# Twelve of sixteen input blocks through the seven products of a Strassen step, and a weight combination made by adding transfers

## The chip, the cores and the metric

The kernel runs on one core of one Trainium2 chip. The metric is the device time in microseconds of one execution; several are run and their median is taken. The core has a matrix engine (TensorE, PE in the profile), a vector engine (VectorE, DVE), an activation engine (ScalarE, ACT), GpSimd (POOL), and SyncE (SP), which here only issues transfers; 16 DMA engines carry them.

## The reference

Two layers over x (256 tokens by 2048 channels). Each has a mixer, a dense MLP and a gated per-layer embedding:

```python
def squared_relu_mlp(u, w1, w2):
    hdn = jnp.square(jax.nn.relu(jnp.einsum("bsd,df->bsf", u, w1)))
    return jnp.einsum("bsf,fd->bsd", hdn, w2)
...
    h = x
    for i in range(DEPTH):
        ...
        h = h + m                       # mixer A (layer 0) or B (layer 1)
        h = h + squared_relu_mlp(rmsnorm(h, norm_mlp[i]), mlp_w1[i], mlp_w2[i])
        h = h + per_layer_embedding(h, p[i], norm_ple[i], ple_w_proj[i], ple_w_gate[i])
    return rmsnorm(h, norm_final)
```

D_MODEL is 2048, D_FF 8192, SEQ 256, all in float32. The change concerns the product u @ w1 of both layers' MLPs.

## The kernel before

**Precision by splitting.** Every float32 weight tile is split into a high part (float32r) and the rest: ScalarE copies the tile into `whi` (line 1044), VectorE subtracts that from the tile into `wlo` (line 1559), and TensorE multiplies three times, high by high, high by low and low by high (`three`, lines 711 to 713). A weight tile of two blocks (256 rows by 512 columns) is called a slot here; `whi` and `wlo` are rings of four slots. TensorE counts `slot_used` up after each slot, ScalarE may write slot i only when TensorE has finished slot i - 4, VectorE follows ScalarE (`slot_hi`), TensorE follows VectorE (`slot_lo`). All engines go through the slots in the same order, which is written out by hand.

**The MLP.** The hidden dimension is cut into 8 chunks of 1024 columns. Chunk 0 of u @ w1 is computed in two plain blocks of 8 half-steps each (`up.b` and `up.b + 1`). Then 7 steps (`FIRST`, then `STEP` six times) each compute the next chunk of u @ w1 and, in the same slots, the down product of the previous chunk with w2; `END` does the last down product. With two layers there are 14 such steps.

**Seven products.** In a step, the 2 by 2 arrangement (two token halves; two halves of the input blocks; two halves of the chunk's columns) of 8 of the 16 input blocks goes through Strassen's seven products in Winograd's form. A slot `("m", of, part)` is product `of` with the weight blocks 2*part and 2*part + 1: 2 blocks of one token half, 6 matmuls. The other 8 input blocks go in `("r", column half, part)`, and the down products in `("d", column block, part)` and `("e", 3, part)` (the last column block of the chunk before): 2 blocks of both token halves, 12 matmuls. `STEP` has 38 slots: 14 "m", 12 "d", 4 "e", 8 "r", which is 372 matmuls of 128x512. `FIRST` has 34 slots, without the "e".

**Weight combinations.** Products 5, 6, 7 and 4 need sums of the four quarters of w1's chunk. The quarters lie in `raw` as four fields, loaded with 1 MB each by `field`; VectorE makes each combination in place, part by part (`weight_sum`, line 1570), at a slot that `sums_after` gives: eight instructions of 128x1024 a step. All other slots are loaded by `plain` into a ring of four buffers `pl`, each reload waiting for the `slot_lo` of its last use.

**What VectorE has beside the split.** Before a slot's split, `run_step` places other work by the slot's index: the turned hidden blocks (`turn_hidden`, index `HIDDEN1` and `hidden_before`), the low part of hidden operands (`HI0`, `HI1`), the addition of a finished down column block to `h` (`add_down`, 4 slots after its last slot), and `mix` (4 instructions on PSUM, lines 1577 to 1583), 5 slots after the last of products 6 and 7:

```python
                        if i == t.at("d", j, 3) + SLOTS:
...
                            add_down(base + t.at("d", j, 3) + 1, j)
                    if i == corners_done(t) + SLOTS + 1:
                        mix(t, base, n)
...
                slot_low(layer, k, parity, i, raw[:, FIELD[of], 2 * part:2 * part + 2, :] if kind == "m" else
...
                for later in t.sums_after(i):
                    weight_sum(t, n, later)
```

**Combinations of u.** Four sums of the input blocks are made once a layer by `combine` in `run_mlp`, between the slots of `up.b + 1`: `whole` (high and low parts added up, line 1640, 128x2048), four sums of 128x512, their high parts on ScalarE and the low parts on VectorE. The low parts of `up.b` and `up.b + 1` come from line 1388, their matmuls from lines 678 to 680.

Of the kernel before, what the change touches and what calls it, by code (L numbers as in the profile page):

```python
# [36 lines left out]
SP_TILES = 4  # L37
LATE = (("d", 2, 0), ("m", 2, 0), ("d", 2, 1), ("m", 2, 1), ("d", 2, 2), ("d", 2, 3),
        ("m", 4, 0), ("r", 0, 0), ("m", 4, 1), ("r", 0, 1), ("r", 0, 2), ("r", 0, 3),
        ("m", 3, 0), ("r", 1, 0), ("m", 3, 1), ("r", 1, 1), ("r", 1, 2), ("r", 1, 3))  # L40
FIRST = (("m", 1, 0), ("m", 1, 1), ("d", 0, 0), ("d", 0, 1), ("m", 5, 0), ("d", 1, 0), ("m", 5, 1), ("d", 1, 1),
         ("m", 7, 0), ("m", 6, 0), ("m", 7, 1), ("d", 0, 2), ("d", 0, 3), ("m", 6, 1), ("d", 1, 2), ("d", 1, 3)) + LATE
# [13 lines left out]
SUMS = (5, 6, 7, 4)  # L56
FIELD = {1: 0, 5: 0, 6: 0, 4: 0, 7: 1, 3: 2, 2: 3}
COMBO = {5: 0, 6: 1, 7: 2, 3: 3}
BANK = {1: 0, 2: 0, 7: 1, 4: 1, 5: 2, 3: 2, 6: 3}
IN_PLACE_AFTER = {5: 1, 6: 5, 7: None, 4: 6}  # L60
OUT_ADD, OUT_TURN = (17, 19), (17, 21)
HI0, HI0_END, HIDDEN1, HI1, HI1_FIRST, HI1_END = 6, 4, 3, 12, 11, 12
# [7 lines left out]
class Table:  # L70


    def __init__(self, slots):
        self.slots = tuple((s + (None,))[:4] for s in slots)
        plain = [s[:3] for s in self.slots if s[0] != "m"]
        self.loads = tuple(dict.fromkeys(plain))
        self.load = tuple(None if s[0] == "m" else self.loads.index(s[:3]) for s in self.slots)
# [20 lines left out]
FIRST, STEP, END = Table(FIRST), Table(STEP), Table(END)  # L98

# [5 lines left out]
def field_freed(t):  # L105
    return t.at("m", 4, 1), t.at("m", 7, 1), t.at("m", 3, 1), t.at("m", 4, 1)
# [1962 lines left out]
```

## Time and profile before

| | us |
|---|---|
| median of 3 runs | 2232.65 (2230.52 to 2233.39) |
| the profiled execution, its own time | 2228.94 |
| its span | 2227.2 |
| TensorE busy | 2204.0 (99%) |
| VectorE busy | 1720.9 (77%) |
| ScalarE busy | 1243.1 (56%) |
| granted TensorE clock, mean | 0.998 |
| DMA | 503.56 MB, 226 GB/s over the span |

Busy time is that in which an engine runs an instruction. A matmul's row gives 0.39 us, but matmuls overlap: the next one starts 0.23 us later, and it is the distance between starts that adds up. The same holds in a small way on VectorE: an instruction of 1.22 us is followed by the next 1.13 to 1.14 us after its start.

### The profile page before, as it was taken

What the parts mean: (1) busy time and instruction counts of PE and PEld (TensorE: products, weight loads), DVE (VectorE), ACT (ScalarE), POOL (GpSimd) and SP (SyncE); (2) the same over time, 40 slices, a digit from 0 to 9 for tenths busy, and PEclk for the clock granted to TensorE, in tenths of its full rate; (3) what the DMA queues carried; (4) which work ended last, traced back from release to release, by engine and by line L of the source; (5) the groups of instructions that cost most, each with busy time, mean ns of one, the idle gap of its engine ahead of it and who ended that gap; (6) DMA issues with size and microseconds to landing.
All of it is one profiled execution on the core that took longest, in us unless ns stands there. A gap on an engine that the chain in (4) does not pass through costs nothing.

```text
span 2227.2 us, 29440 instructions
## 1 busy us (share of the span) xinstructions
PE 2204.0 (99%) x10152; PEld 1832.7 (82%) x10152; DVE 1720.9 (77%) x1897; ACT 1243.1 (56%) x1542; POOL 156.9 (7%) x183
## 2 busy tenths in 40 slices
PE   8999999999999999999999999999999999999998
PEld 7998688888888888887888888888888888888876
DVE  6999868787787787767766667688877877877676
ACT  5666656556556556456744444565564554654565
POOL 3888000000000000000000000000000000000000
PEclk9999999999999999999999999999999999999999
DMA  9544498768677677688876777777776776776783
GB/s 341 171 152 152 140 317 245 242 210 243 222 212 242 219 216 236 223 230 256 236 251 194 244 239 218 251 237 253 214 239 219 216 235 218 224 227 224 232 263 139
DMA packets 499528, 503.56 MB, mean 226 GB/s; under 512 B 261040, under 2 KB 299120, under 8 KB 498416
## 3 DMA queue, kind: packets, MB, share of 16 engines
q1 hardware_dynamic: 497600, 499.71, 72.3%
q10 hardware_dynamic: 1696, 1.67, 0.2%
q8 instruction: 50, 0.82, 0.2%
q0 software_dynamic: 144, 1.05, 0.1%
q14 instruction: 38, 0.31, 0.0%
HBM read 464.62 MB, written 37.75 MB: 226 GB/s over the span
## 4 chain that ended last, share of the span: by engine, by line
PE 75%; DVE 4%; DMA 3%; ACT 1%; issue 1%; SPq 1%; DVEq 0%; ACTq 0%
PE acc L711 14%; PE acc L713 13%; PE acc L712 13%; PE acc L678 7%; PE acc L680 7%; PE acc L679 7%; PE tp L711 4%; PE tp L713 4%; PE tp L712 4%; DMA pT<-staged 2%; DVE wlo L1559 1%; DMA staged<-prows 1%; SPq L430 1%; DVE prows L1473 1%; DVE wlo L1388 1%
## 5 line engine op out<-in xcount | busy, mean ns | idle before, releaser
L1044 ACT ACTIVATE whi<-pl 128x1024 fp32r<-128x1024 f32 x372 | 386.5, 1049 | 303.1 <-PE acc L713 207.0
L1559 DVE TENSOR_TENSOR wlo<-pl,whi 128x1024 fp32r<-128x1024 f32 x372 | 442.8, 1205 | 142.5 <-ACT whi L1044 137.1
L1388 DVE TENSOR_TENSOR wlo<-raw,whi 128x1024 fp32r<-128x1024 f32 x248 | 296.4, 1220 | 128.7 <-ACT whi L939 125.3
L939 ACT ACTIVATE whi<-raw 128x1024 fp32r<-128x1024 f32 x248 | 255.8, 1054 | 198.2 <-PE acc L680 186.4
L1044 ACT ACTIVATE whi<-raw 128x1024 fp32r<-128x1024 f32 x196 | 207.3, 1058 | 184.6 <-PE acc L713 121.7
L1559 DVE TENSOR_TENSOR wlo<-raw,whi 128x1024 fp32r<-128x1024 f32 x196 | 238.5, 1219 | 54.8 <-ACT whi L1044 51.1
L678 PE MATMUL acc<-whi,b_hi 128*128 128x512 f32 x672 | 262.4, 390 | 2.1 <-DVE wlo L1388 1.6
L679 PE MATMUL acc<-wlo,b_hi 128*128 128x512 f32 x672 | 261.5, 389 | 0.0
L680 PE MATMUL acc<-whi,b_lo 128*128 128x512 f32 x672 | 261.5, 389 | 0.0
L711 PE MATMUL acc<-whi,a_hi 128*128 128x512 f32 x596 | 232.3, 390 | 0.6 <-DVE wlo L1559 0.6
L711 PE MATMUL acc<-whi,b_hi 128*128 128x512 f32 x596 | 232.2, 390 | 0.7 <-DVE wlo L1559 0.7
L713 PE MATMUL acc<-whi,b_lo 128*128 128x512 f32 x596 | 231.9, 389 | 0.0
L712 PE MATMUL acc<-wlo,a_hi 128*128 128x512 f32 x596 | 231.9, 389 | 0.0
L713 PE MATMUL acc<-whi,a_lo 128*128 128x512 f32 x596 | 231.9, 389 | 0.0
L712 PE MATMUL acc<-wlo,b_hi 128*128 128x512 f32 x596 | 231.9, 389 | 0.0
L678 PEld LDWEIGHTS acc<-whi,b_hi 128*128 128x128 f32 x672 | 126.2, 188 | 30.2 <-issue 3.2
L680 PEld LDWEIGHTS acc<-whi,b_lo 128*128 128x128 f32 x672 | 126.2, 188 | 26.4
L679 PEld LDWEIGHTS acc<-wlo,b_hi 128*128 128x128 f32 x672 | 126.2, 188 | 26.2 <-issue 0.2
L1570 DVE TENSOR_TENSOR raw<-raw 128x1024 f32<-128x1024 f32 x112 | 136.1, 1215 | 0.0
L711 PEld LDWEIGHTS acc<-whi,b_hi 128*128 128x128 f32 x596 | 111.9, 188 | 25.4 <-DVE wlo L1559 1.4
L711 PEld LDWEIGHTS acc<-whi,a_hi 128*128 128x128 f32 x596 | 111.9, 188 | 25.4 <-DVE wlo L1559 1.5
L713 PEld LDWEIGHTS acc<-whi,b_lo 128*128 128x128 f32 x596 | 111.9, 188 | 23.3
(218 smaller groups left out, 4049.7 us busy)
## 6 DMA issues: line engine op xcount, KB each, us to landing
pl<-in_mlp_w SPq DMA_DIRECT2D x368, 512.0 KB, 5.0
raw<-in_mlp_w SPq DMA_DIRECT2D x72, 1024.0 KB, 6.0
raw<-in_sc_w_in SPq DMA_DIRECT2D x48, 1024.0 KB, 6.4
raw<-in_cf_w_pw SPq DMA_DIRECT2D x64, 512.0 KB, 8.7
raw<-in_ple_w_gate SPq DMA_DIRECT2D x32, 1024.0 KB, 7.4
staged<-prows SPq DMA_DIRECT2D x240, 128.0 KB, 3.3
pT<-staged SPq DMA_DIRECT2D x56, 512.0 KB, 5.8
raw<-in_cf_w_pw SPq DMA_DIRECT2D x16, 1024.0 KB, 7.4
```

The source lines that it names most:

```text
L430: nc.sync.dma_start(rows[:, :, i * Q:(i + 1) * Q], turned[i * Q:(i + 1) * Q, :, :]).then_inc(staged_ready, 16)
L678: nc.tensor.matmul(o, xhi[:, k, s], hi, start=first and c == 0, stop=False)
L679: nc.tensor.matmul(o, xhi[:, k, s], lo, start=False, stop=False)
L680: mm = nc.tensor.matmul(o, xlo[:, k, s], hi, start=False, stop=last and c == 1)
L711: nc.tensor.matmul(o, xhi, hi, start=start, stop=False, skip_group_check=again)
L712: nc.tensor.matmul(o, xhi, lo, start=False, stop=False, skip_group_check=again)
L713: return nc.tensor.matmul(o, xlo, hi, start=False, stop=stop, skip_group_check=again)
L939: nc.scalar.activation(whi[:, e % SLOTS, :, :], raw[:, e // 2, 2 * (e % 2):2 * (e % 2) + 2, :], ACT.Copy).then_inc(hi_ready, 1)
L1044: nc.scalar.activation(whi[:, ring(parity, i), c, :], source[:, c, :], ACT.Copy).then_inc(slot_hi, 1)
L1388: nc.vector.tensor_tensor(wlo[:, e % SLOTS, :, :], raw[:, e // 2, 2 * (e % 2):2 * (e % 2) + 2, :], whi[:, e % SLOTS, :, :].bitcast(F32), A ...
L1559: nc.vector.tensor_tensor(wlo[:, ring(parity, i), c, :], source[:, c, :], whi[:, ring(parity, i), c, :].bitcast(F32), ALU.subtract).then_i ...
L1570: nc.vector.tensor_tensor(o, x, y, ALU.subtract).then_inc(slot_sum, 1)
```

## The change

Twelve of the 16 input blocks go through the seven products (`SP_TILES` from 4 to 6: three parts for each product), four are left for "r". A `STEP` then has 42 slots: 21 "m", 13 "d" (the last down tile is given as two single slots of 6 matmuls each), 4 "e", 4 "r". The order is written anew. w1's quarters are loaded in parts of 512 KB into `raw` (the last part into `vpad`); the fourth quarter comes through the plain ring. The signs are turned so that each combination is a running addition: 5 is b11 + b12 (VectorE), 6 adds b22 to it, 4 adds b21 (VectorE), 7 is b12 + b22 (VectorE). The addition for product 6 is made by three transfers of 512 KB a step that GpSimd issues with an adding write (`add_block`), each after the split of product 5's slot; ScalarE waits for them (`t2_ready`). `whole` is 128x3072 now and is made in `up.b` after its first split (`gather`); the sums of u are 128x768, their high and low parts are made in pieces. `mix` keeps its four instructions with other signs, and its place by rule: 5 slots after the last of products 6 and 7.

```diff
-SP_TILES = 4
-LATE = (("d", 2, 0), ("m", 2, 0), ("d", 2, 1), ("m", 2, 1), ("d", 2, 2), ("d", 2, 3),
-        ("m", 4, 0), ("r", 0, 0), ("m", 4, 1), ("r", 0, 1), ("r", 0, 2), ("r", 0, 3),
-        ("m", 3, 0), ("r", 1, 0), ("m", 3, 1), ("r", 1, 1), ("r", 1, 2), ("r", 1, 3))
...
-STEP = (("m", 1, 0), ("e", 3, 0), ("m", 1, 1), ("e", 3, 1), ("m", 5, 0), ("e", 3, 2), ("m", 5, 1), ("e", 3, 3),
-        ("d", 0, 0), ("m", 6, 0), ("d", 0, 1), ("m", 6, 1), ("d", 0, 2), ("d", 0, 3),
-        ("d", 1, 0), ("m", 7, 0), ("d", 1, 1), ("m", 7, 1), ("d", 1, 2), ("d", 1, 3)) + LATE
+SP_TILES = 6
+SP_PARTS = SP_TILES // 2
+LATE = (("m", 2, 0), ("d", 2, 0), ("m", 2, 1), ("d", 2, 1), ("m", 2, 2), ("d", 2, 2),
+        ("m", 4, 0), ("d", 2, 3), ("m", 4, 1), ("r", 0, 0), ("m", 4, 2), ("r", 0, 1),
+        ("m", 3, 0), ("r", 1, 0), ("m", 3, 1), ("r", 1, 1), ("m", 3, 2))
+FIRST = (("m", 1, 0), ("m", 1, 1), ("d", 0, 0), ("m", 1, 2), ("d", 0, 1), ("m", 5, 0), ("d", 1, 0), ("m", 5, 1),
+         ("d", 1, 1), ("m", 5, 2), ("m", 7, 0), ("m", 7, 1), ("m", 7, 2), ("d", 0, 2), ("m", 6, 0), ("d", 0, 3),
+         ("m", 6, 1), ("d", 1, 2), ("m", 6, 2), ("d", 1, 3, 0), ("d", 1, 3, 1)) + LATE
+STEP = (("m", 1, 0), ("e", 3, 0), ("m", 1, 1), ("e", 3, 1), ("m", 1, 2), ("e", 3, 2), ("m", 5, 0), ("e", 3, 3),
+        ("m", 5, 1), ("d", 0, 0), ("m", 5, 2), ("d", 0, 1), ("m", 7, 0), ("d", 1, 0), ("m", 7, 1), ("d", 1, 1),
+        ("m", 7, 2), ("d", 0, 2), ("m", 6, 0), ("d", 0, 3), ("m", 6, 1), ("d", 1, 2), ("m", 6, 2),
+        ("d", 1, 3, 0), ("d", 1, 3, 1)) + LATE
...
-SUMS = (5, 6, 7, 4)
...
+SUMS = (5, 7, 4)
...
-HI0, HI0_END, HIDDEN1, HI1, HI1_FIRST, HI1_END = 6, 4, 3, 12, 11, 12
+HI0, HI0_END, HIDDEN1, HI1, HI1_FIRST, HI1_END = 8, 4, 3, 15, 13, 12
...
-            if i == max(n - 3, 0 if user is None else self.at("m", user, part)):
+            if i == (self.at("m", 2, part) if of == 4 else max(n - 3, 0 if user is None else self.at("m", user, part))):
...
 def corners_done(t):
-    return max(t.at("m", 6, 1), t.at("m", 7, 1))
+    return max(t.at("m", 6, SP_PARTS - 1), t.at("m", 7, SP_PARTS - 1))
...
 def hidden_before(t):
-    return t.at("r", 0, 3) + SLOTS
+    return t.at("r", 0, 1) + SLOTS
...
+            def field(layer, k, f, part):
+
+                row, col = (SP_TILES if f == 2 else 0) * P + part * 2 * P, NB if f else 0
...
+                nc.sync.dma_start(field_part(f, part), t_in["mlp_w1"][layer][row:row + 2 * P, bass.ds(col, NB)]
+                                  .rearrange("(c r) n -> r c n", r=P)).then_inc(field_ready[f][part], 16)
...
-                free = freed(layer, k, i)
+                    kind, of, part, _ = t.slots[i]
+                    free = freed(layer, k, i) + (t.slots[i][:2] == ("m", 2))
...
+                    if kind == "m" and of in LAST_USE:
+                        sp.wait_ge(slot_lo, free)
+                        if then is not END:
+                            field(layer, k + 1, LAST_USE[of], part)
...
+                elif of == 6:
+                    act.wait_ge(t2_ready[part], 16 * n + 16)
...
             def weight_sum(t, n, i):
 
                 _, of, part, _ = t.slots[i]
...
+                b11, b12, b22 = (field_part(f, part) for f in range(3))
+                b21 = pl[:, t.load[t.at("m", 2, part)] % 4, :, :]
+                o, more, needs = {5: (b11, b12, 1), 7: (b12, b22, 2), 4: (b11, b21, None)}[of]
+                if needs is not None:
+                    dve.wait_ge(field_ready[needs][part], 16 * n + 16)
+                nc.vector.tensor_tensor(o, o, more, ALU.add).then_inc(slot_sum, 1)
...
+                def gather(e):
+                    if e == 0:
+                        dve.wait_ge(operand_ready, 2 * prev.o + 6)
...
+                        steps.mark(nc.vector.tensor_tensor(whole, X[u][0][:, 0:2 * SP_TILES, :].bitcast(F32),
+                                                           X[u][1][:, 0:2 * SP_TILES, :].bitcast(F32), ALU.add))
...
-                run_behind(up.b, Result(prev, BLOCKS - 1), X[u], ROW_MLP + layer, (NORM_MLP[layer], up.s))
+                run_behind(up.b, Result(prev, BLOCKS - 1), X[u], ROW_MLP + layer, (NORM_MLP[layer], up.s), gather)
...
+            def add_block(layer, k, part):
+
+                row, col = (SP_TILES + 2 * part) * P, (k + 1) * 2 * NB + NB
+                pool.wait_ge(slot_lo, first_slot(layer, k) + slots_of(k).at("m", 5, part) + 1)
+                nc.gpsimd.dma_start(field_part(0, part), t_in["mlp_w1"][layer][row:row + 2 * P, col:col + NB]
+                                    .rearrange("(c r) n -> r c n", r=P), accum_op=ALU.add).then_inc(t2_ready[part], 16)
```

## Rows read from the trace of the kernel before

**Rows 1.** The page, busy time of each engine.

```profile
PE 2204.0 (99%) x10152; PEld 1832.7 (82%) x10152; DVE 1720.9 (77%) x1897; ACT 1243.1 (56%) x1542; POOL 156.9 (7%) x183
```

**Rows 2.** Waits of TensorE: line, what it waited for, us in total, times, longest.

```profile
PE acc L678 <- DVE wlo L1388: 4.7, 6, 1.7
...
PE acc L711 <- DVE wlo L1559: 1.4, 2, 0.7
```

**Rows 3.** One STEP: us; busy PE, PEld, DVE, ACT, POOL; clock, DMA share, GB/s.

```profile
574.72:659.39 84.67, 84.65 (x373) 69.67 (x373) 67.57 (x62) 47.39 (x50) 0.00 (x0) 1.00 0.73 224
```

**Rows 4.** Groups of VectorE in that window: the weight combinations.

```profile
L1570 DVE TENSOR_TENSOR raw<-raw 128x1024 f32<-128x1024 f32 x8 | 9.7, 1211 | 0.0
```

**Rows 5.** Timeline of TensorE: first matmul of three slots (m, d, m and on).

```profile
568.20 0.39 PE L711 MATMUL tp<-whi,b_hi 128*128 128x512 f32 x1
...
570.92 0.39 PE L711 MATMUL acc<-whi,s_hi 128*128 128x512 f32 x1
...
572.28 0.39 PE L711 MATMUL tp<-whi,b_hi 128*128 128x512 f32 x1
```

**Rows 6.** Timeline of ScalarE, the same place.

```profile
572.48 1.06 ACT L1044 ACTIVATE whi<-raw 128x1024 fp32r<-128x1024 f32 x1 [0.30 <-PE acc L713]
```

**Rows 7.** Timeline of VectorE around a mix.

```profile
573.58 1.23 DVE L1559 TENSOR_TENSOR wlo<-raw,whi 128x1024 fp32r<-128x1024 f32 x1
574.72 0.68 DVE L1577 TENSOR_TENSOR work<-acc,work 128x512 f32<-128x512 f32 x1
...
577.38 1.22 DVE L1559 TENSOR_TENSOR wlo<-pl,whi 128x1024 fp32r<-128x1024 f32 x1
578.51 1.22 DVE L1588 TENSOR_TENSOR h<-tp,h 128x1024 f32<-128x1024 f32 x1
579.64 1.22 DVE L1559 TENSOR_TENSOR wlo<-raw,whi 128x1024 fp32r<-128x1024 f32 x1
```

**Rows 8.** Timeline of TensorE: a wait in layer 0's FIRST, and the matmul after.

```profile
396.69 0.47 PE L711 MATMUL acc<-whi,b_hi 128*128 128x512 f32 x1 [0.74 <-DVE wlo L1559]
396.99 0.40 PE L712 MATMUL acc<-wlo,b_hi 128*128 128x512 f32 x1
```

**Rows 9.** Timeline of VectorE at that wait.

```profile
395.32 2.36 DVE L1559 TENSOR_TENSOR wlo<-pl,whi 128x1024 fp32r<-128x1024 f32 x2
```

**Rows 10.** Timeline of VectorE at the start of a STEP: the split of slot 3.

```profile
622.96 1.17 DVE L1559 TENSOR_TENSOR wlo<-pl,whi 128x1024 fp32r<-128x1024 f32 x1
```

**Rows 11.** Timeline of TensorE: the start of that slot 3.

```profile
624.29 0.40 PE L711 MATMUL tp<-whi,b_hi 128*128 128x512 f32 x1
```

**Rows 12.** Timeline of VectorE at the start of layer 0's MLP.

```profile
328.72 3.50 DVE L1388 TENSOR_TENSOR wlo<-raw,whi 128x1024 fp32r<-128x1024 f32 x3 [0.47 <-ACT whi L939]
...
338.26 4.63 DVE L1388 TENSOR_TENSOR wlo<-raw,whi 128x1024 fp32r<-128x1024 f32 x4 [1.24 <-ACT whi L939]
...
351.00 2.28 DVE L1640 TENSOR_TENSOR pl<-a_hi,a_lo 128x2048 f32<-128x2048 f32 x1
```

**Rows 13.** Timeline of TensorE there: the half-steps 0 and 3 of up.b.

```profile
330.09 0.47 PE L678 MATMUL acc<-whi,a_hi 128*128 128x512 f32 x1 [0.27 <-DVE wlo L1388]
...
339.63 0.47 PE L678 MATMUL acc<-whi,a_hi 128*128 128x512 f32 x1 [1.10 <-DVE wlo L1388]
```

**Rows 14.** Timeline of VectorE at the start of layer 1's MLP.

```profile
1449.91 1.23 DVE L1431 TENSOR_TENSOR res<-acc,h 128x1024 f32<-128x1024 f32 x1 [0.34 <-PE acc L680]
...
1454.64 3.50 DVE L1388 TENSOR_TENSOR wlo<-raw,whi 128x1024 fp32r<-128x1024 f32 x3 [1.24 <-ACT whi L939]
```

**Rows 15.** DMA issues on the page: KB each, median us from issue to landing.

```profile
pl<-in_mlp_w SPq DMA_DIRECT2D x368, 512.0 KB, 5.0
...
emb_kept<-emb SPq DMA_DIRECT2D x8, 512.0 KB, 12.4
```

**Rows 16.** Landing times of the loads by line 530 in two windows: 569 to 590, and 612.5 to 615.

```profile
DMA to landing us min/median/max: 3.6/4.4/5.4
...
DMA to landing us min/median/max: 6.6/7.1/7.5
```

More of the change, by code:

```diff
@@ L70, with __init__ @@
 class Table:
-    def __init__(self, slots):
+    def __init__(self, slots, single_loads=False):
         self.slots = tuple((s + (None,))[:4] for s in slots)
-        plain = [s[:3] for s in self.slots if s[0] != "m"]
-        self.loads = tuple(dict.fromkeys(plain))
-        self.load = tuple(None if s[0] == "m" else self.loads.index(s[:3]) for s in self.slots)
+        keys = [None if s[0] == "m" and s[1] != 2 else s if single_loads else s[:3] + (None,) for s in self.slots]
+        self.loads = tuple(dict.fromkeys(key for key in keys if key is not None))
+        self.load = tuple(None if key is None else self.loads.index(key) for key in keys)
         self.freed = tuple(max(i for i, n in enumerate(self.load) if n == m) for m in range(len(self.loads)))
@@ L387, in trunk @@
         u2_ready, u3_ready, mixed = sem("u2_ready"), sem("u3_ready"), sem("mixed")
+        t2_ready = [sem(f"t2_ready{p}") for p in range(SP_PARTS)]
         up_free, down_free = sem("up_free"), sem("down_free")
@@ new lines, in plain @@
+            def plain(layer, k, n, free=None):
+                kind, of, part, single = slots_of(k).loads[n]
+                tiles = slice(0, 2) if single is None else slice(single, single + 1)
+                down = kind in "de"
+                w = t_in["mlp_w2" if down else "mlp_w1"][layer]
+                row, col = (((k - (kind == "e")) * 2 * NB, of * NB) if down else
+                            (2 * SP_TILES * P, (k + 1) * 2 * NB + of * NB) if kind == "r" else (SP_TILES * P, (k + 1) * 2 * NB))
+                row, rows = row + (2 * part + tiles.start) * P, (tiles.stop - tiles.start) * P
+                src = (w[bass.ds(row, rows), col:col + NB] if down else w[row:row + rows, bass.ds(col, NB)]
+                       ).rearrange("(c r) n -> r c n", r=P)
@@ L563, in load_step @@
                         take_back(c1)
-                        if t is FIRST:
-                            field(layer, 0, 3)
                     if i == hidden_before(t) - 1:
@@ L1642, in combine @@
+                def combine(e):
+                    if e == 0:
                         steps.wait()
-                        a11, a12, a21, a22 = (whole[:, k:k + TILES, s:s + P] for s in (0, P) for k in (0, TILES))
-                        s1, s2, s3, s4 = (combos[:, i, :, :] for i in range(4))
-                        steps.mark(nc.vector.tensor_tensor(s1, a21, a22, ALU.add))
-                        nc.vector.tensor_tensor(s3, a11, a21, ALU.subtract)
+                        steps.mark(nc.vector.tensor_tensor(s1, a21, a22, ALU.subtract))
@@ L1894, in short_taps @@
                 dve.wait_ge(vpad_ready, 32 * j + 32)
+                dve.wait_ge(const_ready, 4)
                 for k in range(WB):
@@ L2043, in _ @@
             nc.gpsimd.dma_start(bias2, t_in["cf_b_pw2"][0].partition_broadcast(P)).then_inc(bias2_ready, 16)
+            def add_block(layer, k, part):
[3 more added lines that the diff above has]
+                                    .rearrange("(c r) n -> r c n", r=P), accum_op=ALU.add).then_inc(t2_ready[part], 16)
+            for layer in range(DEPTH):
+                for k in range(STEPS):
+                    for part in range(SP_PARTS):
+                        add_block(layer, k, part)
+                if layer == 0:
+                    pool.wait_ge(slot_lo, first_slot(0, STEPS))
+                    nc.gpsimd.memset(vpad[:, :, 0:PAD], 0.0).then_inc(const_ready, 1)
 _INS = ["x", "p", "norm_mix", "norm_mlp", "norm_ple", "cf_w_pw1", "cf_b_pw1", "cf_w_dw", "cf_b_dw",
```

167 lines of the change are left out of this document (90 added, 77 removed).

## Prediction

> **What bounds the kernel now.** I read the busy times first, to see whether one engine fills the span: TensorE is busy 2204.0 of 2227.2 us [rows 1]. Then TensorE's waits, to see what the rest is: it waits 1.4 us in all in the MLP's slots [rows 2]. So a matmul taken away there is worth its full distance, if the slots still come in time. Then one STEP by itself: 84.67 us, clock 1.00, VectorE busy 67.57 of them, ScalarE 47.39, DMA share 0.73 [rows 3]. VectorE is second, with 17 us to spare over 38 slots; what counts is whether they lie where they are needed, since TensorE can run no more than three slots ahead of a late split. Last the timelines, for distances. An "m" slot takes 1.36 us and a "d" slot 2.72, six and twelve times 0.2267 [rows 5]. ScalarE starts a slot 0.20 us after TensorE ends the slot four before it, VectorE's split starts 1.30 us after that end [rows 5 to 7]. TensorE starts 1.37 us after the start of its split: 338.26 to 339.63 and 395.32 to 396.69 [rows 8, 9, 12, 13]; a wait also costs about 0.09 us more, as the second matmul comes after 0.30 and not 0.23 us [rows 8]. Back to back, VectorE's split, combination or addition to h takes 1.135 us (577.38, 578.51, 579.64), and a mix 2.66 us (574.72 to 577.38) [rows 7].
>
> **The matmuls.** "m" goes from 14 to 21 slots (84 to 126 matmuls), "r" from 8 to 4 (96 to 48): 372 to 366 in a STEP, 324 to 318 in FIRST. Six times 0.2267 is 1.36 us a step, 14 steps: -19.0 us.
>
> **VectorE and ScalarE over a step.** Slots go from 38 to 42, but two are halves (one instruction of 512 elements is 0.68 us, line 1577 in [rows 7]). VectorE: two full splits more (2.3), two halves (1.2), combinations from 8 [rows 4] to 6, because product 6's are taken away (2 x 1.135 fewer), and the third parts of 5, 7 and 4 (3 x 1.135 more). That is 40 full and 2 half splits, 9 combinations: in all about +4.6 us, 72 of 83 us. ScalarE gains some 3.3 us and stays near 51. Neither is full on average, so this costs nothing by itself.
>
> **Where VectorE's work falls.** The rule "mix 5 slots after the last corner" now puts it elsewhere. In the new STEP, ("m",6,2) is slot 22; 23 and 24 are half slots, 25 is ("m",2,0), 26 "d", 27 ("m",2,1), 28 "d". Four slots of 1.36 us in a row follow one another just ahead of the mix (27). Take TensorE's start of slot 22 as 0; without waits it starts 25 at 4.08, 26 at 5.44, 27 at 8.16, 28 at 9.52, 29 at 12.24. VectorE can begin slot 25's split at 1.30 (slot 21 ended at 0). Then, each 1.135: split 25; combination for product 4, part 0 (new place: behind ("m",2,part)) at 2.44; split 26 at 3.57 (TensorE can start at 4.94, in time); mix from 4.71 to 7.37; split 27 at 7.37, so TensorE starts it at 8.74 and not 8.16; combination part 1 at 8.50; addition of down block 1 (`add_down`, 4 slots after slot 24) at 9.64; split 28 at 10.77, so TensorE starts it at 12.14. Slot 27 would have been over at 10.10. TensorE falls back 0.58 and then 2.04, together 2.62, plus 0.09 of restart: **2.7 us a step**. Afterwards split 29 at 11.9, combination, split 30 at 14.2 are in time for 14.9 and 16.2. FIRST has the same slots there (mix at 23, addition at 24), so it pays the same. Fourteen times 2.7 is +37.8 us. Before, the mix stood among "d" slots and the row shows VectorE going on without a wait of TensorE [rows 2, 7].
>
> The neighbours of this place bound it. Below: ScalarE runs ahead and doesn't matter; if VectorE's chain of 9.47 us (seven instructions and the mix, less the overlap that the starts already hold) were 2.6 us shorter, nothing would be lost. Above: the same, if a load is late too (below).
>
> **The start of a step** is the other dense stretch. It already runs at the edge: split 3 starts at 622.96, TensorE its slot 3 at 624.29, 1.33 later [rows 10, 11]. In the new order VectorE does 14 instructions from there to slot 11's split (8 splits, 4 combinations, a hidden operand, an addition): 622.96 + 15.9 + 1.37 = 640.2, and TensorE wants slot 11 at 624.29 + 16.32 = 640.6. To slot 15 it is 21 instructions: 648.2 against 648.8. It holds by 0.4 us: no cost, but no room. In FIRST the four "m" in a row (slots 9 to 12) give VectorE a backlog that reaches slot 13 about 0.5 us late; before it was 0.7 at slot 11 [rows 8]. I count that as even. The end of a step (hidden block at slot 40) has the same m, r, m cover ahead of it as before.
>
> **The start of the MLP.** `gather` puts `whole` between splits 0 and 1 of up.b. For 2048 elements it took 2.28 us [rows 12]; for 3072 that makes 3.4. In layer 0 VectorE is already late there: TensorE starts half-step 0 at 330.09, right behind its split (328.72), and waits 1.10 us at half-step 3 [rows 12, 13]. Everything to split 3 moves by 3.4, less some 0.1 of gaps: **+3.3 us**. Behind it nothing makes this good, as TensorE is the bound. In layer 1 the block before ends at about 1449.7, when VectorE's addition starts, and split 3 at 1454.64 is needed only at 1449.7 + 8.16 - 1.37 = 1456.5 [rows 14]; the addition is pushed back by about 0.9 us, which is hidden. The later sums of u (four of 768, their low parts in pieces) cost VectorE about what the old ones did.
>
> **The adding transfers.** Product 5's part is split about 11 us into a STEP, and product 6's is needed by ScalarE at about 30 and at the latest at 34: 19 to 23 us for 512 KB; in FIRST it is 12 to 15. The trace has no adding transfer. From below it is a plain load of that size, 5.0 us, from above the copy of `emb` out, 12.4 us [rows 15]. It reads its target too, so I take about 8. All of this is hidden, so +0. The Trainium skill, "DMA: Bandwidth & Descriptors", section "Anatomy of one DMA — SWDGE (gpsimd) path", gives 2.0 us plus bytes over 436 GB/s, an estimate of 3.2 us here; the load row's 5.0 is more, and by either the sum is the same.
>
> **GpSimd** is idle in the MLP (156.9 us busy in all, [rows 1]); its queue holds only these issues, and each waits for a split that comes anyway.
>
> **SP and the buffers.** Nine field parts replace four 1 MB loads. Around the dense place a reload waits for its slot's split: ("m",2,2)'s load goes out when split 26 is done (4.8), ("d",2,3)'s when split 28 is done (12.0); the latter lands at 12.1 + L, is copied, split, and lets slot 32 start at about 14.7 + L, wanted at 20.3. It is in time for L up to 5.6. Loads in the same part of the old step landed in 3.6 to 5.4 [rows 16]: +0.
>
> **Sum.** -19.0 + 37.8 + 3.3 = +22.1 us. The profiled execution's own time is 2228.94, span 2227.2: it becomes 2251.0. The median of the runs, 2232.65, lies 3.7 above it, so I say **2254.7, about 2254 us**, slower by 1%.
>
> **Rivals.** A change within 0.2% (4.5 us) could hardly be told from none.
>
> 1. The cut is realised. The burst at slots 25 to 28 is absorbed, because VectorE's distances are shorter there, or TensorE has more lead than I give it. Needed: the chain to split 28 ends by 8.15 and not 10.77. Then -19.0 + 3.3: 2217. For it: before, no STEP shows a wait. Against: the distances are those of rows of the same instructions.
> 2. Half of the burst is absorbed (1.3 us a step instead of 2.7): 2232.65 - 19.0 + 18.2 + 3.3 = 2235, between 2225 and 2245.
> 3. The transfers become the bound at the same place. The adding ones bring 1.57 MB more to 84.67 x 224 = 19.0 MB, or twice that if the target's read counts: share 0.73 x 84.67 = 61.8 us busy, plus 5 to 10, over 86: 0.78 to 0.84. If loads then land as slowly as those beside the staged exchange, 7.1 us and up to 8 [rows 16], ("d",2,3) is 1.5 to 2.4 us late each step: 21 to 34 us more, 2276 to 2288. Against it: the adding transfers run in the first half of the step, the tight loads in the second. The Trainium skill, same page, section "Issuing engines are not separate DMA queues", says that transfers of all issuers share the same 16 engines; by that rule GpSimd's queue brings no relief, and no run here shows it yet.
> 4. An adding transfer takes over 23 us: each step waits at product 6. At 12.4 this is far off; beyond 2290.
>
> **Chances.** Forecast 0.60 (own range 2245 to 2265); rival 1 0.13; rival 2 0.11; rivals 3 and 4 0.16. The range 2230 to 2286 leaves out rival 1, a part of rival 2 and the end of 3 and 4, about 0.2. Slower: 0.60 + 0.16 + half of rival 2 = 0.81; same 0.04; faster 0.15.
>
> **What would show it.** Right: TensorE waits on line 1559's successor about 14 to 28 times, twice a step at ("m",2,1) and the "d" behind it, 2.6 us a step; the distance from mix to mix near 86.0 us; VectorE without a gap from ("m",2,0) to split 28; layer 0's up.b with a wait of about 1.7 us at half-step 1 and 2.9 at half-step 3. Wrong: steps of 83.3 us; ScalarE waiting for a transfer, by name, at product 6 or at `pl`; or waits of TensorE at slots 4 to 15, which would say that the start of the step is the tighter place.

## Result: slower by 1.6%, and the profile after

The changed kernel took 2266.95 us (median of 4 runs, 2258.89 to 2275.96), the kernel before 2232.3 us beside it (4 runs, 2230.52 to 2233.39): a ratio of 1.0157 [1.0108, 1.0206]. It is slower, as forecast, and within the range of 2230 to 2286, but 13 us above the forecast of 2254, and 2 us outside the band of 2245 to 2265 that had got a chance of 0.60. The change cost 34.7 us and not 22.1. Its runs also spread over 17 us, those of before over 3. The profiled execution is the slowest of the four (2275.96 us), so its trace shows more trouble than the median has.

The page of the changed kernel: busy times, the queues that are new or will matter, and the issues of the adding transfers (KB each, median us to landing). The answers to [rows 1] and [rows 15]:

```profile
span 2274.2 us, 29838 instructions
...
PE 2205.6 (97%) x10068; PEld 1820.6 (80%) x10068; DVE 1790.1 (79%) x1975; ACT 1289.4 (57%) x1606; POOL 207.2 (9%) x226
...
q0 software_dynamic: 11568, 23.07, 5.6%
...
q8 instruction: 59, 0.97, 0.2%
...
pl<-in_mlp_w SPq DMA_DIRECT2D x340, 512.0 KB, 5.1
...
raw<-in_mlp_w POOLq DMA_DIRECT2D x42, 512.0 KB, 9.5
```

The waits of TensorE (line, what for, us in total, times, longest), which answer to [rows 2]:

```profile
PE acc L730 <- DVE wlo L1593: 37.8, 34, 3.7
PE acc L697 <- DVE wlo L1422: 9.0, 6, 2.7
PE acc L732 <- issue: 3.3, 1, 3.3
```

84 matmuls are gone and TensorE is busy for no less time (2205.6 us, before 2204.0). It now waits 37.8 us for VectorE's splits in the slots, where it waited 1.4. And once it stands for 3.3 us though nothing that the profile shows is missing.

One step, from mix to mix (columns as in [rows 3]); VectorE's timeline around the mix (start, us, as in [rows 7]); and TensorE's two waits there:

```profile
426.02:511.74 85.72, 83.61 (x367) 68.46 (x366) 71.93 (x67) 50.46 (x55) 3.56 (x3) 1.00 0.82 239
```

```profile
593.99 1.23 DVE L1593 TENSOR_TENSOR wlo<-pl,whi 128x1024 fp32r<-128x1024 f32 x1 [2.46 <-ACT whi L1068]
595.13 1.22 DVE L1605 TENSOR_TENSOR raw<-raw,pl 128x1024 f32<-128x1024 f32 x1
596.27 1.22 DVE L1593 TENSOR_TENSOR wlo<-pl,whi 128x1024 fp32r<-128x1024 f32 x1
597.40 0.68 DVE L1612 TENSOR_TENSOR work<-acc,work 128x512 f32<-128x512 f32 x1
...
600.06 1.21 DVE L1593 TENSOR_TENSOR wlo<-pl,whi 128x1024 fp32r<-128x1024 f32 x1
601.19 1.22 DVE L1605 TENSOR_TENSOR raw<-raw,pl 128x1024 f32<-128x1024 f32 x1
602.33 1.22 DVE L1623 TENSOR_TENSOR h<-tp,h 128x1024 f32<-128x1024 f32 x1
603.46 2.35 DVE L1593 TENSOR_TENSOR wlo<-pl,whi 128x1024 fp32r<-128x1024 f32 x2
```

```profile
601.33 0.50 PE L730 MATMUL acc<-whi,a_hi 128*128 128x512 f32 x1 [0.31 <-DVE wlo L1593]
...
604.73 0.50 PE L730 MATMUL acc<-whi,b_hi 128*128 128x512 f32 x1 [1.74 <-DVE wlo L1593]
```

This is the forecast burst: from split 25 (593.99) to split 28 (603.46) VectorE has no gap, 9.47 us as worked out, and TensorE is late at slot 27 and again at slot 28. The step takes 85.7 to 85.8 us in place of 84.4 (the mean between the mixes of before), +1.34: 1.36 us fewer for six matmuls, 2.70 us more for the burst.

The start of layer 0's MLP, VectorE and TensorE (answers to [rows 12, 13]):

```profile
331.08 1.22 DVE L1422 TENSOR_TENSOR wlo<-raw,whi 128x1024 fp32r<-128x1024 f32 x1 [0.46 <-ACT whi L963]
332.22 3.35 DVE L1675 TENSOR_TENSOR pl<-a_hi,a_lo 128x3072 f32<-128x3072 f32 x1
...
343.89 2.36 DVE L1422 TENSOR_TENSOR wlo<-raw,whi 128x1024 fp32r<-128x1024 f32 x2 [1.25 <-ACT whi L963]
```

```profile
336.86 0.47 PE L697 MATMUL acc<-whi,a_hi 128*128 128x512 f32 x1 [1.40 <-DVE wlo L1422]
...
345.26 0.47 PE L697 MATMUL acc<-whi,a_hi 128*128 128x512 f32 x1 [2.73 <-DVE wlo L1422]
```

From split 0 to split 3 it is 12.81 us, before 9.54: +3.27, forecast 3.3.

**What the forecast did not have.** The hidden operand is written out and read back turned (`pT<-staged`). In layer 0's FIRST it comes back late: the transfer's landing time (the queue from 393.9 to 394.6), then ScalarE, then TensorE:

```profile
pT<-staged SPq DMA_DIRECT2D x1, 512.0 KB, 11.1
```

```profile
405.26 1.06 ACT L1021 ACTIVATE b_hi<-pT 128x1024 fp32r<-128x1024 f32 x1 [4.40 <-DMA pT<-staged]
```

```profile
408.92 0.77 PE L730 MATMUL acc<-whi,b_hi 128*128 128x512 f32 x1 [3.74 <-DVE wlo L1593]
409.49 0.63 PE L731 MATMUL acc<-wlo,b_hi 128*128 128x512 f32 x1
409.91 0.63 PE L732 MATMUL acc<-whi,b_lo 128*128 128x512 f32 x1
...
411.62 0.46 PE L730 MATMUL acc<-whi,b_hi 128*128 128x512 f32 x1
```

The return was issued at 394.11 and used at 405.26, eleven us later. Layer 1's FIRST has the same again: the return lands in 11.0 us, ScalarE waits 2.7 us for it, and TensorE then waits 2.1:

```profile
1538.90 1.06 ACT L1021 ACTIVATE a_hi<-pT 128x1024 fp32r<-128x1024 f32 x1 [2.74 <-DMA pT<-staged]
```

```profile
1542.57 0.47 PE L730 MATMUL acc<-whi,a_hi 128*128 128x512 f32 x1 [2.09 <-DVE wlo L1593]
```

After the wait at 408.92 the matmuls come every 0.43 us and not every 0.227: the clock's lower level, 1.2 GHz, for about 3 us. The same fall follows some other waits. Ahead of the last 10 us, the windows of 5 us in which the mean clock is below 0.97 begin in this trace at 15, at 405 and 410, at 1055, at 1910 and from 1940 to 1950; the trace of before has none but at its end. And in layer 1 one step took 95.3 us. In it (TensorE's timeline; the code queue from 1930 to 1950):

```profile
1941.38 0.49 PE L730 MATMUL acc<-whi,b_hi 128*128 128x512 f32 x1 [1.86 <-DVE wlo L1593]
...
1946.09 0.59 PE L732 MATMUL acc<-whi,b_lo 128*128 128x512 f32 x1 [3.29 <-issue]
1946.47 0.63 PE L730 MATMUL tp<-whi,a_hi 128*128 128x512 f32 x1
```

```profile
q8 instruction: 4, 0.07, 1.4%
```

TensorE stops ahead of the last matmul of a step's slot 0, when its inputs are there, in a stretch in which four packets of code arrive; then the clock is low to about 1950.7. The step is the first behind a jump back of TensorE's loop.

### The profile page after: what moved, and what is told of

It is laid out like the page before. It is cut to its first block, busy times and chain, and to the rows that moved or that the text cites. A ratio compares the mean times of both kernels' runs of the same rounds, so it can differ in the third digit from the quotient of the medians.

```text
span 2274.2 us, 29838 instructions
## 1 busy us (share of the span) xinstructions
PE 2205.6 (97%) x10068; PEld 1820.6 (80%) x10068; DVE 1790.1 (79%) x1975; ACT 1289.4 (57%) x1606; POOL 207.2 (9%) x226
## 4 chain that ended last, share of the span: by engine, by line
PE 62%; DVE 9%; DMA 7%; issue 3%; ACT 3%; SPq 1%; DVEq 0%; ACTq 0%
PE acc L730 11%; PE acc L732 11%; PE acc L731 11%; PE acc L697 6%; PE acc L698 6%; PE acc L699 6%; PE tp L730 3%; PE tp L732 3%; PE tp L731 3%; DVE wlo L1593 3%; DMA pT<-staged 3%; DMA staged<-prows 2%; SPq L442 1%; ACT whi L1068 1%; DVE raw L1605 1%
## 5 line engine op out<-in xcount | busy, mean ns | idle before, releaser
L1593 DVE TENSOR_TENSOR wlo<-pl,whi 128x1024 fp32r<-128x1024 f32 x372 | 431.5, 1165 | 155.6 <-ACT whi L1068 154.8
L1422 DVE TENSOR_TENSOR wlo<-raw,whi 128x1024 fp32r<-128x1024 f32 x248 | 296.8, 1220 | 129.6 <-ACT whi L963 126.1
L963 ACT ACTIVATE whi<-raw 128x1024 fp32r<-128x1024 f32 x248 | 255.8, 1054 | 194.7 <-PE acc L699 188.5
L1593 DVE TENSOR_TENSOR wlo<-raw,whi 128x1024 fp32r<-128x1024 f32 x238 | 289.8, 1220 | 21.1 <-ACT whi L1068 13.9
L1068 ACT ACTIVATE whi<-raw 128x1024 fp32r<-128x1024 f32 x238 | 251.3, 1057 | 82.8 <-PE acc L732 57.9
L699 PE MATMUL acc<-whi,b_lo 128*128 128x512 f32 x672 | 261.6, 389 | 0.0
L698 PE MATMUL acc<-wlo,b_hi 128*128 128x512 f32 x672 | 261.6, 389 | 0.0
L730 PE MATMUL acc<-whi,a_hi 128*128 128x512 f32 x568 | 223.9, 394 | 17.6 <-DVE wlo L1593 17.6
L732 PE MATMUL acc<-whi,b_lo 128*128 128x512 f32 x568 | 222.0, 391 | 3.3 <-issue 3.3
L732 PE MATMUL acc<-whi,a_lo 128*128 128x512 f32 x568 | 222.1, 391 | 0.0
L731 PE MATMUL acc<-wlo,a_hi 128*128 128x512 f32 x568 | 221.9, 391 | 0.0
L731 PE MATMUL acc<-wlo,b_hi 128*128 128x512 f32 x568 | 221.8, 391 | 0.0
L2100 POOL DMA_DIRECT2D raw<-in_mlp_w x42 | 50.1, 1193 | 1680.2 <-DVE wlo L1593 1680.2
L699 PEld LDWEIGHTS acc<-whi,b_lo 128*128 128x128 f32 x672 | 126.2, 188 | 26.2
L697 PE MATMUL acc<-whi,a_hi 128*128 128x512 f32 x320 | 125.6, 393 | 6.8 <-DVE wlo L1422 6.8
```

Of the source, the lines that this page charges most:

```text
L697: nc.tensor.matmul(o, xhi[:, k, s], hi, start=first and c == 0, stop=False)
L698: nc.tensor.matmul(o, xhi[:, k, s], lo, start=False, stop=False)
L699: mm = nc.tensor.matmul(o, xlo[:, k, s], hi, start=False, stop=last and c == 1)
L730: nc.tensor.matmul(o, xhi, hi, start=start, stop=False, skip_group_check=again)
L731: nc.tensor.matmul(o, xhi, lo, start=False, stop=False, skip_group_check=again)
L732: return nc.tensor.matmul(o, xlo, hi, start=False, stop=stop, skip_group_check=again)
```

## Experiments

Each is the changed kernel with the edit shown. Ratios are to the kernel before, run beside it on the same chip (2233.1 us for experiments 1 to 4, 2233.7 for 5 to 8, 2233.0 for 9 to 11, 2233.6 for 12). The changed kernel was run beside another 2232.3, so differences of two experiments from different groups carry about 1 us of that. Where "waits" or "steps" are given, they come from one profiled execution of each kernel.

**1. The addition later.**

```diff
-                            if i == t.at("d", j, 3) + SLOTS:
+                            if i == t.at("d", j, 3) + (2 * SLOTS if j == 1 else SLOTS):
```

> The changed kernel with one edit: the addition of down column block 1 to h stands 8 slots after its last slot (slot 32 of a STEP) and not 4 (slot 28). Theory A, VectorE's burst behind the mix sets the step: split 28 starts 1.135 us earlier, TensorE's second wait shrinks from 1.74 to about 0.6 us, the distance from mix to mix goes from 85.7 to 84.6 us, 14 x 1.13 = 16 us off the whole. Rival T, the transfers set it (ScalarE waits some 4 us a step for the load of product 2's last part): the distance stays at 85.7, as the load's time doesn't change. Rival C, what costs is the TensorE clock's fall after a wait: the gain would be more than 16 us and the spread of the runs would shrink.

2248.29 us (2241.97 to 2251.64), ratio 1.0067 [1.0055, 1.008]. Steps of 84.6 us, 1.15 less:

```profile
PE acc L730 <- DVE wlo L1593: 19.6, 32, 2.5
```

One instruction of VectorE (1.135 us), moved out of the burst by four slots, gives its own length back in each step. The burst sets the step, and there VectorE's time is TensorE's. By medians the gain is 18.7 us, a little more than 14 times 1.15, and the spread fell from 17 to 9.7 us, so rival C has a small part that this run can't exclude. The trace also has a step of 91.9 us, with a stand of 2.7 us.

**2. No adding transfers.** ScalarE's wait for them goes too. The kernel leaves b22 out of product 6, so it is for its time alone.

```diff
-                for k in range(STEPS):
-                    for part in range(SP_PARTS):
-                        add_block(layer, k, part)
```

> The changed kernel without the adding transfers: product 6 takes the combination of product 5 as it is (the output leaves out b22 in product 6). Theory A: the steps stay at 85.7 us from mix to mix. Of the first step of layer 0, which had a TensorE wait of 3.7 us for the staged exchange beside three adding transfers, the wait goes, with the slow clock after it: 4 to 6 us off in all, for both layers up to 8. Rival T: the steps themselves become shorter by 1 us or more, 14 us or more in all, and ScalarE's waits for pl fall from 8 us a step to near 3. If the adding transfers cost nothing at all, the time stays.

2258.03 us (2257.0 to 2259.21), 1.0117 [1.0102, 1.0132]. Steps of 85.7 to 85.8 us, as with them, so inside a step the transfers are hidden, as forecast. But the median is 8.9 us lower, more than theory A's 4 to 8, and the spread 2 us in place of 17 (four runs each). In FIRST the return lands in 6.8 us, in layer 1's in 5.6, and ScalarE finds the operand there, without a wait:

```profile
pT<-staged SPq DMA_DIRECT2D x1, 512.0 KB, 6.8
```

```profile
400.05 1.05 ACT L1021 ACTIVATE b_hi<-pT 128x1024 fp32r<-128x1024 f32 x1
```

**3. The gather later.**

```diff
-                    if e == 0:
+                    if e == 5:
```

> The changed kernel with the sum of high and low parts (128x3072) behind split 5 of up.b and not behind split 0. If its place costs what was forecast, TensorE's waits at half-steps 1 and 3 of layer 0's up.b (about 1.9 and 2.7 us) fall back to one of about 1.1 us: 3.3 us off, layer 1 unchanged. If something else of the start sets the time (the exchange that brings the last input blocks), the 3.3 us are waited for later and the time stays.

2261.78 us (2259.29 to 2265.71), 1.0138 [1.0123, 1.0153]: 5 us below the changed kernel's median, 0.4 us above its fastest run, so four runs each don't decide it. The trace says more: split 0 and split 3 lie 9.54 us apart again (329.14, 338.68), and the waits on line 1422 fall from 9.0 to 6.4 us. But a part of the delay has only moved. At its new place the gather (342.10, 3.35 us) holds up the low part of an operand, and TensorE waits for that:

```profile
350.22 0.50 PE L697 MATMUL acc<-whi,a_hi 128*128 128x512 f32 x1 [1.76 <-DVE a_lo L1527]
```

From the first matmul of line 697 to FIRST, TensorE takes 135.4 us, with the early gather 137.0, before 133.1: the move gives back about half of the 3.3 us (such a stretch differs by up to 1 us from trace to trace), and the rest is waited for at the new place. The low clock at 340 to 350, behind the wait of 2.7 us, stands in four of the seven traces with the early gather (not in the changed kernel's own) and in none of the five with the late one.

**4. A product ahead of the down load,** with edit 1. ("m",6,2) comes before ("d",1,2), and the mix six slots behind it, so a "d" slot more lies inside the burst.

```diff
-         ("m", 6, 1), ("d", 1, 2), ("m", 6, 2), ("d", 1, 3, 0), ("d", 1, 3, 1)) + LATE
+         ("m", 6, 1), ("m", 6, 2), ("d", 1, 2), ("d", 1, 3, 0), ("d", 1, 3, 1)) + LATE
...
-                        if i == corners_done(t) + SLOTS + 1:
+                        if i == corners_done(t) + SLOTS + 2:
```

> Three edits against the burst: the addition of e1; the last part of product 6 stands ahead of the down slot before it (slots 21 and 22 exchanged); the mix 6 slots after it (still slot 27). Theory A, worked out with the same distances: TensorE starts slot 27 on time and slot 28 about 0.1 to 0.2 us late, the distance from mix to mix is 83.5 us, 14 x 2.2 = 31 us off, which is about the time of the kernel before or 10 us below it. Rival T: the load of product 2's last part (issued behind split 26) or the next one is then what TensorE waits for, and the distance stays at 84.5 or more, with ScalarE's wait for pl ahead of TensorE's.

2242.36 us (2231.62 to 2255.98), 1.0052 [1.0029, 1.0075]. Steps of 83.7 us with one wait of 0.3 us:

```profile
PE acc L730 <- DVE wlo L1593: 8.5, 17, 2.1
```

The burst is gone and the fastest run is 1.5 us below the median of the kernel before, and yet this kernel's median is 11 us above its fastest run and the spread 24 us. Against the changed kernel the median fell by 24.6 us where 31 were expected. Something beside the burst and the gather costs, and not in every run.

**5. The combination by VectorE,** with no adding transfers (the edit of experiment 2 as well).

```diff
-SUMS = (5, 7, 4)
+SUMS = (5, 7, 6, 4)
...
-IN_PLACE_AFTER = {5: 1, 7: None, 4: 6}
+IN_PLACE_AFTER = {5: 1, 7: None, 6: 5, 4: 6}
...
-                o, more, needs = {5: (b11, b12, 1), 7: (b12, b22, 2), 4: (b11, b21, None)}[of]
+                o, more, needs = {5: (b11, b12, 1), 7: (b12, b22, 2), 6: (b11, b22, 2), 4: (b11, b21, None)}[of]
```

> The combination for product 6 is made by VectorE in place (b11 plus b22, three more 128x1024 additions a step, behind the splits of slots 15, 17 and 19), and the 42 adding transfers are gone; burst, order and the gather are as in the changed kernel. Theory A (the adding transfers buy VectorE time that it does not need: the step is set by TensorE and by the burst of slots 25 to 28, and the irregular 10 to 17 us come from the transfers): the sums lie in VectorE's slack, the distance between mixes stays 85.7 us, the wait of the first chunk's exchange goes, and the time is 2257 to 2262 us with a spread of under 4 us, as in the run without the adding transfers. Rival B (VectorE needs the relief: 3 x 1.13 = 3.4 us more work a step pushes the burst later): up to 14 x 3.4 = 48 us more, and at least 1 us a step, so 2272 us or more, with waits of TensorE on VectorE's splits at slots 17 to 21.

2262.71 us (2260.07 to 2266.75), 1.0127 [1.0112, 1.0142], steps of 85.7 to 85.8 us. VectorE does 42 instructions more (1834.3 us busy) and no step is longer: the relief that the transfers were to bring was not needed. Theory A missed one thing: the trace has a step of 94.7 us and a stand without any adding transfer.

```profile
PE acc L732 <- issue: 4.6, 1, 4.6
```

So that part does not need the transfers, and the small spread of experiment 2 says less than I had read in it. The return lands in 6.0 and 5.5 us here, and no FIRST has the long wait.

**6. All mends, sum by VectorE** (edits 1, 3, 4, 5).

> All mends together: the sum for product 6 by VectorE, no adding transfers, the gather behind split 5, addition 1 of the down product eight slots later, and load (m,6,2) before (d,1,2) with the mix six slots behind it. Theory A (the terms add): the burst costs 0.3 us a step in place of 2.05 and the gather 1 us in place of 3.3, so the time is the cut of 84 matmuls with little given back: 2214 to 2224 us, 0.4 to 0.8% below the kernel before, with a spread of under 4 us. Rival B (VectorE, at 85% and with three more additions in a step, is late again at slots 20 to 28): the step stays above 84.4 us and the time is 2232 us or more.

2232.76 us (2226.84 to 2242.89), 1.0005 [0.9993, 1.0017]: theory A's time is missed by 9 us. The profiled run, its fastest, has steps of 83.6 to 83.8 us, 0.72 below before, and no fall of the clock ahead of the end; the other runs lose up to 16 us more. But even this run is 3 us above theory A. Its twelve steps from mix to mix are 8.7 us shorter than before's in all, its span only 2.2. The rest goes outside them: 2.0 us from line 697's first matmul to FIRST (135.1 against 133.1, see experiment 3), 2.4 us in FIRST and END of the two layers, where the cut alone makes 1.5 less, and about 2 us before, between and behind the two MLPs' steps. The same stretches differ by up to 1 us between the kernel before and experiment 11.

**7. All mends, adding transfers kept** (edits 1, 3, 4).

> The same mends with the adding transfers kept. Theory A (the transfers cost by being there): its fastest run comes within 3 us of the kernel without them, near 2225 to 2230 us, but the runs spread over more than 10 us and the median is 5 to 15 us above it. Rival B (the spread of the runs so far is chance): spread and median as in the kernel with the sum by VectorE, 2214 to 2224 us.

2238.38 us (2229.07 to 2248.68), 1.0024 [1.0006, 1.0042]; steps 83.7. The median is 5.6 us above experiment 6, with runs of the two (twelve each) that overlap widely. In layer 0's FIRST ScalarE waits 4.3 us for the operand, TensorE 3.7, and the clock falls; in layer 1's it is 3.0 and 2.3 us, and the clock falls again.

**8. The same transfers, copying and not adding.** Product 6 gets b22 alone, so this kernel too is for its time only.

```diff
-                                    .rearrange("(c r) n -> r c n", r=P), accum_op=ALU.add).then_inc(t2_ready[part], 16)
+                                    .rearrange("(c r) n -> r c n", r=P)).then_inc(t2_ready[part], 16)
```

> The changed kernel with the same 42 transfers from GpSimd's queue, of the same size, at the same places and behind the same waits, but copying b22 over b11 in place of adding to it (so product 6 is multiplied by b22 alone). Theory A (it is the adding, which reads its target as well as writing it): time and spread fall to those without any of these transfers, 2257 to 2260 us with 2 to 4 us of spread, the first chunk's exchange lands in 6 to 7 us again. Theory B (it is the traffic or the queue, whatever the transfer does): 2259 to 2276 us with a spread of 10 us or more, the exchange lands in 9 to 11 us, and the landing of the transfers themselves is the same 9.5 us as of those that add.

2260.04 us (2255.84 to 2268.91), 1.0113 [1.0098, 1.0128].

```profile
L2100 POOL DMA_DIRECT2D raw<-in_mlp_w x42 | 29.9, 713 | 1693.1 <-DVE wlo L1593 1693.1
...
raw<-in_mlp_w POOLq DMA_DIRECT2D x42, 512.0 KB, 6.7
```

Between the theories. The copy lands in 6.7 us and not 9.5, an issue takes 713 ns and not 1193, the operand's return lands in 9.2 us in both layers and not in 11, and ScalarE's wait in FIRST is 1.1 us and not 4.4: adding is what makes the transfer heavy, and the copy alone still delays the return. But the spread is 13 us, and the trace has a stand of 4.4 us and a step of 93.2 us, so the median says nothing about adding by itself.

**The operand's return.** All twelve traces of the changed kernel and of its variants have it once in each layer's FIRST.

| transfers from GpSimd | traces | return lands in, us | TensorE's wait behind it, us: layer 0, layer 1 |
|---|---|---|---|
| adding | 7 | 10.3 to 11.7 | 1.5 to 3.8, 1.6 to 2.5 |
| copying | 1 | 9.2 | none of 1.3 or more |
| none | 4 | 5.5 to 6.8 | none of 1.3 or more |

**The code.** Packets on the first code queue, the longest step of layer 1, and the stand of TensorE in it (steps are the distances between the seven mixes of a layer):

| kernel | packets | longest step | stand |
|---|---|---|---|
| before | 50 | 84.4 | none |
| changed | 59 | 95.3 | 3.3 |
| 1 | 59 | 91.9 | 2.7 |
| 2, 3 | 50, 50 | 85.8, 86.0 | none |
| 4, 6, 7 | 50, 50, 50 | 83.9, 83.8, 84.0 | none |
| 5 | 59 | 94.7 | 4.6 |
| 8 | 59 | 93.2 | 4.4 |

In those four steps the first matmul of slot 0 is already 1.2 to 1.9 us late, by the trace on a split of VectorE.

In TensorE's loop the code of the body arrives while it runs for the first time, a packet every 20 to 40 us, and none in the iterations after (for the kernel before 390 to 600 us, then none until 960). In the four traces with 59, the code arrives once more in the second or third iteration of layer 1's loop, its first four packets within 20 to 30 us around the stand, and the stand is each time in slot 0 right behind the jump back. That gave the last experiments: write the loop out.

**9. TensorE's loop written out.**

```diff
-                with pe.Fori(0, STEPS // 2) as it:
+                for it in range(STEPS // 2):
```

> The changed kernel with TensorE's loop over pairs of chunks written out (six steps one after the other, the same matmuls, waits and order; the other engines keep their loops). Theory A (the step of layer 1 that took 95.4 us in the changed kernel, and 91.9 to 94.7 us in three of the experiments, is TensorE waiting for its own code after the jump back: these four traces have 59 packets on the first code queue, the five without such a step 50): no jump, so no step above 86.5 us in the trace, no stand without a shown wait, the packets of that queue rise to 70 or more since all six steps are loaded, and the runs above 2268 us go: 2255 to 2264 us. Rival B (the stand has another cause, such as the staging transfers that are issued in the same microseconds): one step of 92 to 95 us in about half of the runs, and a spread of 10 us or more, 2259 to 2276 us. Rival C: loading all code costs by itself, 1 to 3 us a step, 2265 us or more.

2263.92 us (2262.1 to 2266.71), 1.0138 [1.0123, 1.0154]; 72 packets, no step above 86.0, no stand. The spread falls from 17 us to 4.6, the highest run from 2276 to 2267. The median falls by 3.0 us and the fastest run is 3.2 us slower, so with four runs each only the loss of the longest times shows.

**10. All mends, sum by VectorE, loop written out** (6 and 9).

> The kernel with all mends (2226.8 to 2242.9 us, median 2232.8) with TensorE's loop written out. Theory A: its steps stay at 83.7 us, the runs that are 8 to 16 us above its fastest go, and the time is 2224 to 2230 us, 0.2 to 0.4% below the kernel before. Rival B (the spread is the clock falling after short waits, which no code layout changes): median 2230 to 2234 us and the same 10 to 16 us of spread.

2227.42 us (2226.13 to 2230.51), ratio 0.9978 [0.9969, 0.9987]: faster than the kernel before by 0.22%, with 4.4 us of spread where experiment 6 had 16. The chip doesn't explain that: the kernel before spread over 5.4 us beside this one and over 7.8 beside experiment 6. The page, the waits and a step:

```profile
q8 instruction: 72, 1.18, 0.2%
```

```profile
PE acc L730 <- DVE wlo L1593: 8.2, 21, 0.7
PE acc L697 <- DVE wlo L1422: 6.3, 5, 2.1
```

```profile
502.70:586.40 83.70, 83.39 (x367) 68.56 (x367) 75.25 (x70) 50.47 (x55) 0.00 (x0) 1.00 0.76 226
```

**11. Control: the kernel before, loop written out.**

> Control: the kernel before with TensorE's loop written out. Theory A (in the kernel before the jump back costs nothing, its trace has 50 code packets and steps of 84.4 us throughout): same time within 0.1%, 2230 to 2235 us. Rival C (code that is loaded afresh in every step costs by itself): 5 us or more slower, with steps above 84.7 us.

2233.99 us (2231.3 to 2235.55), 1.0001 [0.9992, 1.001], 73 packets, the same steps. Written out or not makes no difference where the loop's code stays.

**12. All mends, adding transfers kept, loop written out** (7 and 9).

> The mends with the adding transfers kept (2229.1 to 2248.7 us, median 2238.4) and TensorE's loop written out; against the same kernel with the sum by VectorE and the loop written out (2227.4 us, 2226.1 to 2230.5) it differs in the 42 adding transfers alone. Theory A (the transfers cost the wait for the first chunk's exchange, 2 to 4 us with the clock's fall behind it, once in each layer at most, and nothing in the steps): 2230 to 2236 us with under 8 us of spread, steps of 83.7 us. Rival B (they also make the spread): 10 us of spread or more and a median of 2236 us or more. Rival C (they cost nothing once the loop is written out): 2226 to 2230 us.

2233.79 us (2229.94 to 2241.07), 1.0004 [0.9995, 1.0013]. Against experiment 10, which differs only in who makes the combination: 6.4 us. The steps are the same (83.6 to 83.7 in layer 0); the trace has a wait of 3.8 us in layer 0's FIRST and one of 2.2 in layer 1's, with low clock behind both. The median is theory A's. The spread of 11 us is more than A gave and is rival B's.

## Why the prediction was right, and where it was short

The direction, the burst and the range were right. That the median fell inside the range is in part due to the range's width: one term that stood at nothing and one event that was not in the sum together cost about 9 us, beside the 22 that were forecast.

**The cut** (-1.36 us a step, -19.0): right. Before 84.41 us a step; with the burst out of the way (experiment 10) 83.67, that is -1.36 and about 0.6 for the one wait left (0.3 us as shown, and as much again for the later start and the slow second matmul).

**The burst** (2.7 us a step, +37.8): right in its place, its instructions and its size. VectorE's chain took 9.47 us as worked out, mixes lie 85.75 us apart (forecast 86.0, where I had added to the 84.67 of the one step shown, the longest of the twelve), TensorE waits twice. Experiments 1 and 4 took it away in two steps, 1.15 and 0.9 us each. This refutes rivals 1 and 2 for the kernel as changed.

**The gather** (+3.3): right in the trace, 3.27. Not forecast was that the clock can fall behind the wait of 2.7 us, some 1.7 us more.

**FIRST** (as a step, "I count that as even"): short. In the trace of experiment 2, which has no adding transfers, FIRST and END of the two layers are 5.9 us longer than before; the cut and the burst make that 2.7.

**The start of a step** (holds by 0.4 us): right, no wait there; even three more combinations (experiment 5) made none.

**The adding transfers** (+0): the step that failed. "All of this is hidden, so +0" looked at when the transfer lands: 9.5 us, forecast about 8, well within 12 to 23. Inside a STEP they cost nothing, but for 0.3 us in one step of layer 1 in every trace that has transfers from GpSimd. I did not ask what they do to others. In layer 0's FIRST they run while the hidden operand is on its way back, at a DMA share of 1.05 (394 to 402 us) where experiment 2 has 0.71 at the same place (391 to 399). The return lands in 11.1 us and not 6.8, and ScalarE waits for it. The tight transfer was the operand's, not their own, and it is late in both layers: in the changed kernel TensorE waits 3.7 and 2.1 us, and with the fall of the clock (1.7) and the longer step (0.3) that is 7.8 us. By medians they cost 6.4 us (10 against 12), 5.6 (6 against 7), 4.2 (5 against the changed kernel) and 8.9 (2 against it); all four point the same way, but only the first is clear of the runs' noise by itself. The other pairs run TensorE's loop as a loop, so that the code's second arrival may be in them too. Rival 3 had the right kind of trouble at the wrong place: the DMA share of a step is 0.82, as it said (0.78 to 0.84), and ScalarE does wait for `pl` loads (134.1 us in 65 waits), but ahead of the burst, where TensorE doesn't feel it. Of that rival's page of the Trainium skill ("DMA: Bandwidth & Descriptors", section "Issuing engines are not separate DMA queues") the runs now say: by its rule, transfers from GpSimd's queue share the engines with SP's and bring no relief, and the trace agrees, with the return of the operand 4.3 us later beside them (11.1 and 6.8). The fit that the same page of the Trainium skill gives in its section "Anatomy of one DMA — SWDGE (gpsimd) path", an estimate of 3.2 us for 512 KB, was far below the 6.7 us of the plain copy here, with SP's loads running beside it, and the 9.5 us of the adding one.

**Not in the forecast at all:** the second arrival of the loop's code. Its step costs 7.3 to 9.6 us (91.9 against 84.6, 95.3 against 85.75). It was in the changed kernel's profiled run. In the other runs it can only be inferred: writing the loop out lowered the medians by 3.0 us (changed, within noise) and 5.3 (mended, clear of it), and the spread from 17 to 4.6 and 16 to 4.4; none of the longer runs of the mended kernel has a trace. With adding transfers and the loop written out (12) a spread of 11 us is left. Why the code comes again, in some executions and not in others, is open.

**The 13 us** between forecast and median. Experiment 2, whose trace has neither adding transfers nor the second code load, lies 25.0 us above the kernel before, where 22.1 were forecast: 2.9 us are FIRST and the clock behind the gather's wait. The other 9 or so are the adding transfers and the second code load together; how they share it isn't shown, since the second doesn't come in every run.

## What to carry to other kernels

Before an engine that is 77% busy gets the pieces of a tighter order, write out its instructions between two neighbouring slots at the place where the main engine's slots are shortest: here 84 matmuls fewer gained 19 us, and a stretch of 9.5 us in each step, late by 2.6, took 38 back. Work handed to a transfer isn't free because it lands in time; ask which other transfer is tight while it runs. And when a kernel's runs begin to spread, compare the traces' code packets and search the clock for falls, before a theory of the change is asked to explain the median.

## What the runs showed of the hardware

- A wait of TensorE can cost more than itself. Every fall of the clock that the traces show behind the first 20 us and ahead of the last 35 (22 in all) came with a wait or stand of 1.7 us or more (1.75 us ahead of the one at 1910, 2.7 us at 343 to 345, 3.7 us at 405 to 409). 17 of them lasted between 3 and 4 us at 1.2 GHz, which is 1.7 us of full clock lost; the four around a stand for code and the one behind the wait of 3.8 us in experiment 12 lasted about 7 us, twice as much, a part of it while TensorE stood. Most such waits have none behind them: of the 14 burst waits of 1.7 us in the changed kernel, one.
- A transfer of 512 KB that adds to its target in SBUF landed in 9.5 us, one that copies, from the same queue and place, in 6.7 us, and SP's loads in 5.1 us. GpSimd was held 1193 ns by the issue of the one and 713 ns by that of the other. A transfer of SP's queue of the same size took 10.3 to 11.7 us beside adding ones, 9.2 beside copying ones and 5.5 to 6.8 us without either (14, 2 and 8 cases, all in the changed kernel and its variants).
- TensorE can stand 2.7 to 4.6 us in a loop's later iteration while its code is loaded again; 9 packets more on the code queue are the mark of it. It was seen in layer 1's loop only, in 4 of the 9 traces whose kernel runs it as a loop, or 4 of 10 with the kernel before.
